# Projecting the context tokens of latent layer 0 ahead of the image tokens

## The reference

```python
def first_block(...):
    ...
    x = x + mod_x[:, 5, None] * expert_choice_ffn(hx, ...)
    return rms_norm(x, g_final)

def trunk_layer(x, xc, mod, mod_c, ..., with_ctx_out):
    z = split_columns_2((rmsnorm(x, pre_g) * (1 + scale) + shift) @ w_in)
    zc = split_columns_2((rmsnorm(xc, pre_g) * (1 + scale_c) + shift_c) @ w_in)
    ...
```

## Time and profile before

| | |
|---|---|
| median of 3 runs | 2940.76 us (2940.03 to 2942.37) |
| the profiled execution's own time | 2940.52 us |
| its span | 2938.6 us |
| TensorE busy | 2803.2 us, 95% |
| weight loads (PEld) | 2097.7 us, 71% |
| VectorE / ScalarE / GpSimd busy | 35% / 31% / 21% |
| mean granted TensorE clock | 0.983 |

### The profile page before, as it was taken

One profiled execution on the slowest core, in us unless ns is written; L12 is line 12 of the kernel. 1 busy time (PEld: TensorE's weight loads), 2 busy tenths in 40 slices (PEclk: granted clock), 3 DMA queues, 4 the chain that ended last, 5 costly groups with the idle time before them and its releaser, 6 DMA issues.

```text
span 2938.6 us, 37519 instructions
## 1 busy us (share of the span) xinstructions
PE 2803.2 (95%) x15438; PEld 2097.7 (71%) x15438; DVE 1038.2 (35%) x1481; ACT 898.5 (31%) x1365; POOL 614.9 (21%) x295
## 2 busy tenths in 40 slices
PE   6999899999989999999999999999998999999998
PEld 4857777788744333338899567999997878577886
DVE  3436503411341111113375543411135076645114
ACT  5222533422331111104333244211134333344223
POOL 1302031144310000002221002322222241005443
PEclk9999999999999999999999999999998999999999
DMA  6243031122389999992122002111132231003222
GB/s 257 72 197 155 1 137 80 44 100 98 131 333 422 422 422 422 422 421 108 74 76 94 20 1 94 65 65 58 58 115 115 72 109 67 29 4 133 97 90 101
DMA packets 65217, 424.72 MB, mean 145 GB/s; under 512 B 6897, under 2 KB 6897, under 8 KB 18737
## 3 DMA queue, kind: packets, MB, share of 16 engines
q1 hardware_dynamic: 52992, 378.56, 32.8%
q0 software_dynamic: 3664, 24.67, 2.2%
q10 hardware_dynamic: 8416, 19.40, 1.8%
HBM read 405.56 MB, written 17.04 MB: 144 GB/s over the span
## 4 chain that ended last, share of the span: by engine, by line
PE 79%; DMA 8%; DVE 6%; ACT 4%; issue 2%; POOL 1%; SPq 0%; ACTq 0%; DVEq 0%; POOLq 0%
PE psum L700 76%; DMA ring<-in_weights 5%; PE psum L703 3%; DMA late_slots<-in_weights 2%; DVE small L2291 1%; ACT arena L1778 1%; ACT arena L1756 1%; ACT hidden_high L1747 0%; DVE arena L2749 0%; POOL weight_parts L3000 0%; DVE merged_low L2354 0%; ACT hidden L1741 0%; DMA arena<-in_t_count 0%; DVE hidden L2247 0%; ACT weight_parts L1702 0%
## 5 line engine op out<-in xcount | busy, mean ns | idle before, releaser
L700 PE MATMUL psum<-hidden_high,weight_parts 128*128 128x384 f32 (+2 forms) x3296 | 863.7, 362 | 23.1 <-DVE hidden_low L2243 8.3
L3000 POOL TENSOR_TENSOR weight_parts<-ring,weight_parts 128x1024 fp32r<-128x1024 f32 x218 | 546.1, 2507 | 1226.8 <-ACT weight_parts L1702 1226.7
L700 PEld LDWEIGHTS psum<-hidden_high,weight_parts 128*128 128x128 f32 x3296 | 601.5, 189 | 96.9 <-issue 14.6
L700 PE MATMUL psum<-hidden_low,weight_parts 128*128 128x384 f32 (+2 forms) x2160 | 650.3, 361 | 1.2 <-DVE merged_low L2354 0.7
L1702 ACT ACTIVATE weight_parts<-ring 128x1024 fp32r<-128x1024 f32 x218 | 230.5, 1059 | 1016.9 <-PE psum L700 984.9
L700 PE MATMUL psum<-arena 128*64 128x128 f32 (+8 forms) x2992 | 448.1, 358 | 10.1 <-DMA arena<-in_weights 6.5
L700 PEld LDWEIGHTS psum<-hidden_low,weight_parts 128*128 128x128 f32 x2160 | 399.4, 189 | 42.9 <-issue 2.5
L700 PEld LDWEIGHTS psum<-arena 128*64 128x64 f32 (+3 forms) x2992 | 253.7, 155 | 165.1 <-issue 130.2
L1756 ACT ACTIVATE arena<-psum 128x512 f32<-128x512 f32 (+4 forms) x224 | 159.7, 720 | 391.5 <-PE psum L700 374.9
L2372 DVE TENSOR_TENSOR arena<-arena,psum 128x512 f32<-128x512 f32 (+1 forms) x72 | 55.9, 777 | 493.1 <-PE psum L700 492.3
L700 PE MATMUL psum<-ring,arena 128*64 128x512 f32 (+1 forms) x792 | 193.4, 600 | 14.8 <-DMA ring<-in_weights 13.1
(11 more groups left out here) (297 smaller groups left out, 2433.3 us busy)
## 6 DMA issues: line engine op xcount, KB each, us to landing
ring<-in_weights SPq DMA_DIRECT2D x260, 1024.0 KB, 6.9
late_slots<-in_weights SPq DMA_DIRECT2D x48, 1024.0 KB, 15.6
arena<-in_weights SPq DMA_DIRECT2D x48, 1024.0 KB, 17.4
spilled_projections<-arena ACTq DMA_DIRECT2D x14, 384.0 KB, 2.3
arena<-spilled_projections ACTq DMA_DIRECT2D x3, 1536.0 KB, 13.7
residual<-in_acts SPq DMA_DIRECT2D x4, 768.0 KB, 8.3
arena<-in_bias POOLq DMA_DIRECT2D x1, 3072.0 KB, 11.6
arena<-in_t_count POOLq DMA_DIRECT2D x2, 1536.0 KB, 10.4
```

What stands on the lines that cost most here:

```text
L700: return nc.tensor.matmul(o, lhsT, rhs, start=start, stop=stop)
L3000: G_.tensor_tensor(parts[:, i % 2, 1, :], tile_at(t), parts[:, i % 2, 0, :], ALU.subtract).then_inc(*E.sig("tile_split"))
```

## The change

The nine tiles of the block go through the ring twice in layer 0: first as `(name, 0, "c")` over the 256 context tokens (`CTX_ONLY`), then over the 512 image tokens (`IMG`). The context's norm, scale, shift and parting are moved into the last pair of experts; its factors are spread inside the last `exp_down`, into a bank of PSUM that is free there. TensorE's order after `comb` is now: `gq` context, squares of the image, `gk` context, spread for the image, `gv` and `small` context, then all nine tiles over the image. Three `high()` calls stand inside the image's `shift_in`. `keep_warm(5)` behind the squares and `keep_warm(9)` ahead of `gq` are gone from layer 0. All later tiles stand nine places further on in the ring.

```diff
# stream_plan
+        for tag in (("c",), ()) if l == 0 else ((),):
+            out += cols(w, (l,), ("gq", l, *tag), ...) + cols(w, (l,), ("gk", l, *tag), ...)
+            out += rhs(w, (l,), ("gv", l, *tag), B2["gv"], 512)
+            out.append((("small", l, *tag), w, (l,), None, small))
# TensorE, pair(): inside exp_down of the last pair, ahead of tile (e, k) = (0, 6)
+                    if following is None and (e, k) == (0, 6):
+                        pe.wait_ge(*E.upto("combined", 2 + KT * PAIRS))
+                        pe.wait_ge(*E.next("rstd_ready"))
+                        for t in range(2):
+                            ins = mm(psum[:, 7 * 512 + t * P:7 * 512 + (t + 1) * P],
+                                     rstd[:, t:t + 1].to_broadcast([P, P]), C("ident"), True, True)
+                        ins.then_inc(sem("context_spread"), 1)
# TensorE, behind comb
+            pe.wait_ge(*E.next("hidden_ready", KT))
+            for t in range(2):
+                project_tile((("gq", 0, "c"), t), ("gqc", 0, t), CTX_ONLY)
             ps = group("stat", ("pre", 0))
             for k in range(KT):
                 pe.wait_ge(*E.next("norm_squares"))
                 add_up(ps, k, iSq, range(4), finalSquared[:, k, :])
-            keep_warm(5)
+            for t in range(2):
+                project_tile((("gk", 0, "c"), t), ("gkc", 0, t), CTX_ONLY)
             pe.wait_ge(*E.next("rstd_ready"))
-            spread(("pre", 0), 0, range(TT))
+            spread(("pre", 0), 0, range(2, TT))
+            project_tokens([(("gv", 0, "c"), i) for i in range(4)], ("gv", 0), range(2))
+            project_tile(("small", 0, "c"), ("smallc", 0), CTX_ONLY)
...
-                keep_warm(9)
-                project_fresh([(("gq", l), t) for t in range(2)], [("gq", l, t) for t in range(2)], own)
+                if l == 1:
+                    keep_warm(9)
+                project_fresh([(("gq", l), t) for t in range(2)], [("gq", l, t) for t in range(2)], IMG)
# ScalarE, last pair, ahead of eYhi
+                else:
+                    act_(tick[:, 7:8], C("eps"), ACT.Sqrt)
+                    act.wait_ge(*E.taken("stat", "context"))
+                    act_(rstd[:, 0:2], var[:, 0:2], ACT.Sqrt).then_inc(*E.sig("std_ready"))
+                    shift_in(modB[0], 0, CTX_ONLY)
                 act.wait_ge(*E.next("gate_set"))
                 act.wait_ge(*E.written(tag, "exp_down"))
                 act_(eYhi, cols(tag, "exp_down"), ACT.Copy, scale=eGate).then_inc(*E.sig("expert_high"))
# ScalarE, layer 0
+                    shift_in(modB[l], 0, IMG, then=lambda k: high() if k in (1, 3, 5) else None)
+                    evac(("gv", 0, 0), gV[:, 0:2, :]..., n=1024, ahead=True)
+                    evac(("smallc", 0), gSM[:, 0:CTX], n=CTX, ahead=True)
# VectorE, last pair, ahead of eYlo
+                if not following:
+                    inverse(0, 2)
+                    dve.wait_ge(*E.next("context_spread"))
+                    for k in range(KT):
+                        stt(H3[:, k, 0:CTX], R3[:, k, 0:CTX], gmB[:, k, 1:2], psum[:, 7 * 512:7 * 512 + CTX],
+                            ALU.mult, ALU.mult).then_inc(*E.sig("scaled_ready"))
+                    for k in range(KT):
+                        dve.wait_ge(*E.next("hidden_high"))
+                        tt_(Hlo[:, k, 0:CTX], H3[:, k, 0:CTX], Hhi[:, k, 0:CTX], ALU.subtract)\
+                            .then_inc(*E.sig("hidden_ready"))
                 dve.wait_ge(*E.next("expert_high"))
                 stt(eYlo, cols(tag, "exp_down"), eGate, eYhi, ALU.mult, ALU.subtract)\
```

More of the change, by code:

```diff
@@ L101, in stream_plan @@
             out += mod2(1, 1)
-        out += cols(w, (l,), ("gq", l), B2["gq"], 2) + cols(w, (l,), ("gk", l), B2["gk"], 2)
-        out += rhs(w, (l,), ("gv", l), B2["gv"], 512)
         small = np.full(P, -1)
@@ L108, in stream_plan @@
         small[64:96] = B2["kr"] + np.arange(32)
-        out.append((("small", l), w, (l,), None, small))
+        for tag in (("c",), ()) if l == 0 else ((),):
+            out += cols(w, (l,), ("gq", l, *tag), B2["gq"], 2) + cols(w, (l,), ("gk", l, *tag), B2["gk"], 2)
+            out += rhs(w, (l,), ("gv", l, *tag), B2["gv"], 512)
+            out.append((("small", l, *tag), w, (l,), None, small))
         out.append((("decay_w2", l), None, (l,), None, None))
@@ L786, in project_fresh, with project_tokens @@
                 done()
-            def project_tokens(tiles, name):
+            def project_tokens(tiles, name, tokens=range(TT)):
                 ps = []
@@ L794, in project_tokens @@
                         k = 2 * i + j
-                        for t in range(TT):
+                        for t in tokens:
                             if k == 0 and t % 2 == 0:
@@ L1724, in modulation_rows, with token_evac @@
                 ins.then_inc(*E.read(name, "row", b))
-            def token_evac(name, dst):
+            def token_evac(name, dst, first=0):
                 for i in range(3):
                     high()
-                for p in range(TT // 2):
+                for p in range(first, TT // 2):
                     if p == TT // 2 - 1:
@@ L1733, in token_evac, with shift_in @@
                     evac((*name, p), dst[:, 2 * p:2 * p + 2, :].rearrange("p a n -> p (a n)"), n=1024)
-            def shift_in(mod, col, chunks, parted=True):
+            def shift_in(mod, col, chunks, parted=True, then=lambda k: None):
                 for k in range(KT):
                     act.wait_ge(*E.next("scaled_ready"))
+                    if chunks is CTX_ONLY:
+                        act_(H3[:, k, 0:CTX], H3[:, k, 0:CTX], ACT.Identity, bias=mod[:, col + k, 1:2])\
+                            .then_inc(*E.sig("act_step"))
+                        act.wait_ge(*E.own())
+                        act_(Hhi[:, k, 0:CTX], H3[:, k, 0:CTX], ACT.Copy).then_inc(*E.sig("hidden_high"))
+                        continue
                     if chunks is ALL:
@@ L2016, in _ @@
             pair("last", None)
+            high_again()
+            high()
+            high()
             for k in range(KT):
@@ L2028, in _ @@
                         act_(rSqs[:, k, :], R3[:, k, :], ACT.Square).then_inc(*E.sig("norm_squares"))
-                root(("pre", l), pick_tokens(0, TT))
+                if l == 0:
+                    for t in range(2):
+                        evac(("gqc", 0, t), gQ[:, t, 0:CTX], n=CTX, scale=0.125, ahead=True)
+                root(("pre", l), pick_tokens(*((0, TT) if l else (2, 4))))
                 if l == 0:
@@ L2032, in _ @@
                     act_(rstd[:, 8:12], var[:, 2:6], ACT.Sqrt).then_inc(*E.sig("std_ready"))
-                high_again()
-                high()
-                high()
-                act.wait_ge(*E.next("residual_saved", 16))
-                shift_in(modB[l], 0, ALL)
+                    for t in range(2):
+                        evac(("gkc", 0, t), gK[:, t, 0:CTX], n=CTX, ahead=True)
+                    act.wait_ge(*E.next("residual_saved", 16))
+                    shift_in(modB[l], 0, IMG, then=lambda k: high() if k in (1, 3, 5) else None)
+                    evac(("gv", 0, 0), gV[:, 0:2, :].rearrange("p a n -> p (a n)"), n=1024, ahead=True)
+                    evac(("smallc", 0), gSM[:, 0:CTX], n=CTX, ahead=True)
+                else:
+                    high_again()
+                    high()
+                    high()
+                    act.wait_ge(*E.next("residual_saved", 16))
+                    shift_in(modB[l], 0, ALL)
+                every = IMG if l == 0 else ALL
                 for t in range(2):
-                    evac(("gq", l, t), tok_view(gQ[:, t, :], own), own, scale=0.125, ahead=True)
+                    evac(("gq", l, t), tok_view(gQ[:, t, :], IMG), IMG, scale=0.125, ahead=True)
                 for t in range(2):
-                    evac(("gk", l, t), tok_view(gK[:, t, :], ALL), ALL, ahead=True)
-                token_evac(("gv", l), gV)
-                evac(("small", l), tok_view(gSM, ALL), ALL, ahead=True)
+                    evac(("gk", l, t), tok_view(gK[:, t, :], every), every, ahead=True)
+                token_evac(("gv", l), gV, 1 - l)
+                evac(("small", l), tok_view(gSM, every), every, ahead=True)
                 for d in range(2):
@@ L2664, in _ @@
                 E.end(PAIRS - 1)
+            gained(gmB, modB[0], "pre0")
+            dve.wait_ge(*E.next("ctx2_loaded", 16))
             pair("last", False)
@@ L2715, in _ @@
                     post_gain(l)
[L2716 removed]
                     dve.wait_ge(*E.next("residual_ready", 2 * KT))
[L2718 removed]
+                    scale_and_part(("pre", l), lambda k, c: gmC[:, k:k + 1], chunks=IMG)
                 else:
@@ L3052, in _ @@
                 if l == 0:
+                    low(2)
                     pool.wait_ge(*E.next("ctx2_loaded", 16))
@@ L3058, in _ @@
```

(2 more changed lines are left out.)

28 lines of the change are left out of this document (15 added, 13 removed).

## The result

The changed kernel took **2948.98 us** (median of 13 runs, 2945.36 to 2954.42) against 2944.92 for the kernel before (13 runs, 2940.03 to 2949.63). The ratio over all these runs is 1.0018, 95% interval 1.001 to 1.0026, that is +5.3 us with 2.9 to 7.7 as bounds; the medians alone are 4.1 us apart. Forecast was 2944.8, that is +4.0, in the range 2938.5 to 2951. By the 0.2% that the prediction set as its bound this is "the same", at its edge. A second job gave the same kernel 2953.05 us and a ratio of 1.0026 (1.0016 to 1.0036), so the loss is real. One execution of the kernel before, beside the first experiments, took 5576.72 us and is left out of their ratios.

The account below looks back on a forecast made before the run. TensorE was taken as the bound, 101.6 us from the combine to the constants behind `small`. Terms of 100.5 plus 4.25 gave +3.2; +1.5 clock and -0.7 small things made +4.0, so 2944.8 us, range 2938.5 to 2951.

Parts of the forecast that it names:

- Work is not saved: Layer 0's block of nine tiles on TensorE: two passes take 75.1 us, as before (74.6 without waits).
- rival 2: Context products on TensorE: 256 columns don't get shorter, 0.177 us instead of 0.126; +6.1 us, 2950.9; chance 0.05.
- Cost 1, the late combination: Behind the last `exp_down`: ScalarE's context work holds back `eYhi`, so the combine starts 4.25 us later.
- Rival 3: Ahead of the combine: the context is parted in time, so 4.25 us and its gap's clock go; about 2939.5; chance 0.11.
- The terms behind it: TensorE from the combine on: combine, slot, context passes, squares, spread, waits and image pass sum to 100.5 us.
- Cost 2, the parted weights: Around `gv`, `small` and `gq`: TensorE waits 1.6, 0.85, 0.85 and 3.6 us for parted tiles, sum 6.9.
- Rival 4: Context tiles and `gq`: parted tiles also come in time, so the 6.9 us of waits go; 2932.6; chance 0.07.
- The clock of the gaps: Gaps ahead of the combine and `gq`: half clock costs 1.5 us for both together; bounds 0 and 1.5 each.
- Rival 1: TensorE's gaps: clock falls at every gap, three times 1.5 us, and squares run slower; +8.5, 2949.3; chance 0.25.
- Small things: Layer 1's ring wait 0.5 us less, last eviction of `small` 0.2 shorter, nine extra loads 0; together -0.7.
- The sum: Whole kernel: 3.2 + 1.5 - 0.7 = +4.0 us on the execution's 2940.52; median 2944.8.

Follow-up runs that it names:

- the one with the `gq` tiles apart: Changed kernel with layer 0's image pass over the two `gq` tiles going tile by tile, not both k by k: 2944.10 us, ratio 0.9997 to the kernel before.
- the early spread: Changed kernel with the context factors' spread released three k steps earlier in the last `exp_down`: 2947.01 us, ratio 1.0009 to the kernel before.
- The filled gaps: Changed kernel with 7 more constants products in each of TensorE's two long gaps, no wait shortened: 2945.22 us, ratio 1.0004 to the kernel before.
- the run with the highs behind the shift: Changed kernel with ScalarE's three roundings of context weight tiles behind the image shift, not inside it: 2961.73 us, ratio 1.0059 to the kernel before.
- both edits: Changed kernel with the context's spread three k earlier and `gq` image tiles one after another: 2939.41 us, ratio 0.9986 to the kernel before; again 2938.35 us, 0.998.

## Why the prediction was right, and by how much it was short

In order of its steps; "after" is the first profile of the changed kernel.

- **Work is not saved:** held. A `gq` context tile pair is 48 products in 5.74 us, 0.120 each (0.126 foretold), so **rival 2 falls**. The Trainium skill's rule that a weight load overlaps with products only where the row groups differ ("The mechanism", in TensorE: Matmul & The Clock Gate), by which such a product would take 216 ns by the prediction's estimate, is not what this trace shows. The same section names a load into the background weight buffer as a second case that is pulled ahead of products, which the prediction left out.
- **Cost 1, the late combination:** foretold +4.25, measured 22.86 - 17.90 = +4.96. The 0.84 us per k were 0.85. Part of the difference is clock. By the granted clock from `exp_down`'s first product to the combination (rows below: all engines busy in turn, clock behind the five of them; the kernel before and the one with the `gq` tiles apart) 17.90 x 0.08 x 2 = 2.9 us are at half clock before, 22.86 x 0.08 x 2 = 3.7 after, and with the tiles apart 21.57 x 0.03 x 2 = 1.3. Half of that is lost time: less it, the combination starts at 16.5 us before, 21.0 after and 20.9 there. So the term proper is +4.5, and 0.4 is where the half clock of the expert's end happened to fall. With the early spread (19.24 us at a clock of 0.90, so 17.3 without the half clock) 0.9 of it is left, of which 0.7 is the spread itself, 0.71 in the rows; the prediction could leave that out only because TensorE was to wait anyway. **Rival 3** as a forecast falls; as a version, it is what the early spread makes.

```profile
1310.35:1328.25 17.90, 17.67 (x75) 7.77 (x75) 1.74 (x2) 1.11 (x1) 0.00 (x0) 0.92 1.00 417
```

```profile
1310.64:1332.21 21.57, 17.74 (x79) 7.91 (x79) 8.31 (x19) 9.02 (x19) 0.36 (x1) 0.97 0.85 351
```

- **The terms behind it:** combination and slot 5.39 for 4.25; `gq` context 5.74 for 6.05; squares 9.95 for 9.8; `gk` context 7.66 for 8.4; spread 1.02 for 1.2; `gv` and `small` context with their waits 17.33 for 17.2; the wait for `gq` 3.93 for 3.6; image pass 52.66 for 50.0. Sum 103.68, where 100.5 was worked out.
- **Cost 2, the parted weights:** right in size and place, 1.37 + 0.98 + 3.93 = 6.3 for 6.9, but not in every step: the wait ahead of `small` (0.85) did not come. GpSimd took 2.94 us over `gv`'s fourth tile instead of 2.38 (last section), so that tile came late and `small` only 2.99 us behind it, not 3.55. **Rival 4 falls.**
- **The clock of the gaps is the term that was mis-sized.** I took 1.5 us for both long gaps together, reasoning that the first costs less because VectorE's adds pace the combination. The filled gaps show 1.0 + 2.4 = 3.4 us. The bound that I had written down, 1.5 each, was the better value in sum, and even that was too low for the second gap. These 1.9 us too little, and the 0.4 of half clock in `exp_down`, are nearly all of the 2.4 us between the +4.7 foretold for the stretch (4.25 - 1.1 + 1.5) and +7.04.
- **Rival 1** named that mechanism and gave +8.5 for the total. By its own condition, more than 1.9 us lost beyond my sum, it was met in the profiled stretch: 7.04 is 2.4 above 4.7. But its second half is wrong: the squares took 9.95 us, not 11.3, and the short gaps of 1.37 and 0.98 cost no clock (1.00 over 1366.98 to 1385.33). What happened lies between forecast and rival.
- **Small things:** ring wait 0.12 won for 0.5; `small`'s eviction 0.5 for 0.2; the nine extra loads cost nothing that a row shows (no wait for DMA in the stretch; HBM read 410.80 MB for 405.56).
- **The sum:** 7.04 - 0.5 - 0.1 = +6.5 for the change's own places, against a measured +5.3 (2.9 to 7.7) and, in the other job, +7.7 (4.7 to 10.6). The forecast of +4.0 was right in sign, cause and class, and short by about 2.5 us, most of it the clock. That the medians' 4.1 us meet the +4.0 so well is luck. So is the number: the kernel before came out at 2944.92 us over 13 runs and not at the 2940.76 of three, which the forecast was added to. In absolute terms the 2944.8 are 4.2 us too low, and 2948.98 lies beyond the forecast's own range (2942 to 2947.5), though within the whole one.

What the experiments add is that the idea was worth more than it gave. Undoing the two big waits, each with a few lines, turns the loss into a gain: 115.2 us for the stretch against 119.5.

## What to carry to other kernels

Work that is pulled forward to fill an engine's idle time must be asked for its helpers: here sixteen small ScalarE instructions stood in front of one that TensorE waited for and made it some 4.5 us late, and starting them 5 us earlier, where their input had long been ready, cost only the 0.7 us of the spread. Splitting a tile's products over two passes shortens the time in which the next tile can be prepared; where the preparation takes longer than that, start consuming with the first tile that is ready, not when a pair is. A long gap on TensorE is to be priced with what the clock takes behind it: the gaps of 3.83 and 3.93 us cost 1.0 and 2.4 us here, the waits of 1.37 and 0.98 nothing.

## What was not expected of the hardware

**VectorE and GpSimd block each other.** In the changed kernel VectorE's subtraction of two SBUF operands isn't done until GpSimd's own subtraction ends. Timeline of VectorE, then of GpSimd, in the changed kernel:

```profile
1373.94 1.69 DVE L2286 TENSOR_TENSOR hidden_low<-hidden,hidden_high 128x512 fp32r<-128x512 f32 x1 [0.69 <-ACT hidden_high L1769]
1375.55 0.73 DVE L2291 SCALAR_TENSOR_TENSOR hidden<-residual,small,psum 128x512 f32<-128x512 f32 x1
...
1377.47 2.22 DVE L2286 TENSOR_TENSOR hidden_low<-hidden,hidden_high 128x512 fp32r<-128x512 f32 x1
1379.61 0.74 DVE L2291 SCALAR_TENSOR_TENSOR hidden<-residual,small,psum 128x512 f32<-128x512 f32 x1
```

```profile
1372.70 2.38 POOL L3054 TENSOR_TENSOR weight_parts<-ring,weight_parts 128x1024 fp32r<-128x1024 f32 x1 [1.92 <-ACT weight_parts L1717]
1376.20 2.94 POOL L3054 TENSOR_TENSOR weight_parts<-ring,weight_parts 128x1024 fp32r<-128x1024 f32 x1 [1.12 <-ACT weight_parts L1717]
```

GpSimd ends at 1375.08 and 1379.14, VectorE 0.55 us later both times, about the length of one such instruction; GpSimd's second one was held up as well, 2.94 for 2.38, by VectorE's from 1376.21, and so was the one from 1383.45, 2.80, by VectorE's from 1383.32. The form that reads PSUM keeps its 0.73 us. With GpSimd silent the same instruction takes 0.67 to 0.69 (the run with the highs behind the shift). The Trainium skill, SBUF — State Buffer, section "SBUF: two separate sides", says just this of a VectorE instruction with two SBUF inputs against a GpSimd one that reads SBUF; the trace agrees. It seems to have cost the changed kernel nothing: the last `hidden_low` ended at 1384.0, ahead of the parted tile at 1389, and the tile of `small` was parted by 1382.13, just as TensorE came to it. No run shows the same kernel without it.

**The clock's pattern repeats.** The changed kernel's two profiles, taken in different jobs, have the same stretch to 0.03 us, half clock included, and so have the two with both edits to 0.08 us, though one reached it 2.2 us later. But the program alone does not set where it falls: up to the combination the kernel with the tiles apart has the changed kernel's program, and yet its combination started 1.3 us earlier in the stretch, with 1.3 us at half clock instead of 3.7. The 3.4 us at 2446 came and went between kernels as well. A change of a few microseconds is judged wrongly by a total alone; what makes the clock fall at 2446 was not tried.
